# RWKV phase of a two-layer diffusion step: side work, piece copies and the first pair's rows placed anew

## What is computed

```
mod = silu(cond) @ w_ada + b_ada            # 6*D columns, per layer; "ada" chunks of 256 columns
h   = rms_norm(x, g_mix) * (1 + sc1) + sh1
p   = h @ w_in                              # its last 3*D columns are the branch gates
# RWKV-7, forward and backward, 8 heads of 64 (the reference's scan over time):
s   = s*w_t + (s a_t) b_t + v_t k_t ;  y_t = s r_t
gn  = group_norm(y_f + flip(y_b)) * lnx_w + lnx_b
o_c = (gn + bonus) * g_c
gates  = sigmoid(p[..., OFF_GATE:])         # 3 x D
merged = gates[0]*(o_a @ w_po_a) + gates[1]*(o_b @ w_po_b) + gates[2]*(o_c @ w_po_c)
x = x + gt1 * (merged @ w_out)
x = x + gt2 * (swiglu FFN of the normed x)  # uses sh2, sc2, gt2 of mod
```

## Time and profile before

| what | value |
|---|---|
| median of 3 runs | 1980.56 us |
| the profiled execution's own time | 1980.41 us |
| its span, and the mean granted TensorE clock | 1978.5 us, 0.963 |
| PE / DVE / ACT / POOL busy | 90% / 49% / 38% / 14% |
| chain that ended last: PE / DVE / ACT / issue | 74% / 13% / 6% / 4% |
| phase 3 of layer 0 and of layer 1, about | 394 to 637 us, 1364 to 1595 us |

### The profile page before, as it was taken

One profiled execution on the slowest core, in us unless ns is written; L12 is line 12 of the kernel. 1 busy time (PEld: TensorE's weight loads), 2 busy tenths in 40 slices (PEclk: granted clock), 3 DMA queues, 4 the chain that ended last, 5 costly groups with the idle time before them and its releaser, 6 DMA issues.

```text
span 1978.5 us, 42029 instructions
## 1 busy us (share of the span) xinstructions
PE 1781.8 (90%) x18403; PEld 1492.9 (75%) x18403; DVE 963.2 (49%) x1699; ACT 748.9 (38%) x1325; POOL 273.7 (14%) x457
## 2 busy tenths in 40 slices
PE   4899888778897999999989998987788989999998
PEld 2899555437664989999989984554566679899998
DVE  1526436576654463334342454375666446533332
ACT  2434435334335343333233434454333343533321
POOL 2000003265430000000000000052745000000000
PEclk9899998989898999999999999999799999999999
DMA  7443233201305445763442442321031443344342
GB/s 260 163 121 117 81 100 114 81 12 46 109 3 165 157 128 138 191 171 95 132 153 88 128 120 89 123 93 49 2 109 46 128 145 116 98 128 128 102 128 80
DMA packets 268525, 219.51 MB, mean 111 GB/s; under 512 B 7289, under 2 KB 259608, under 8 KB 267704
## 3 DMA queue, kind: packets, MB, share of 16 engines
q1 hardware_dynamic: 264816, 203.67, 34.2%
q0 software_dynamic: 3312, 13.09, 1.9%
q10 hardware_dynamic: 216, 0.06, 0.0%
HBM read 210.77 MB, written 6.03 MB: 110 GB/s over the span
## 4 chain that ended last, share of the span: by engine, by line
PE 74%; DVE 13%; ACT 6%; issue 4%; POOL 1%; DMA 1%; ACTq 0%; SPq 0%; DVEq 0%; POOLq 0%
PE bank L588 13%; PE bank L593 13%; PE bank L589 12%; PE bank L647 8%; PE bank L1256 3%; PE bank L1254 3%; PE bank L1255 3%; PE bank L1029 3%; PE bank L653 2%; PE bank L547 2%; PE bank L644 1%; PE bank L1038 1%; PE bank L774 1%; PE bank L811 1%; PE bank L572 1%
## 5 line engine op out<-in xcount | busy, mean ns | idle before, releaser
L589 PE MATMUL bank<-scr_rounded 128*128 128x384 f32 x1344 | 452.4, 337 | 0.0
L589 PEld LDWEIGHTS bank<-scr_rounded 128*128 128x128 f32 x1344 | 253.7, 189 | 1.3
L647 PE MATMUL bank<-h,ring 128*128 128x384 f32 x576 | 215.9, 518 | 31.0 <-ACT gtmp L1486 14.7
L588 PE MATMUL bank<-scr_rounded 128*128 128x384 f32 (+1 forms) x672 | 226.6, 337 | 13.9 <-ACT scr_rounded L1505 13.3
L588 PE MATMUL bank<-scr_rounded,gate_rounded 128*128 128x384 f32 (+1 forms) x672 | 228.0, 339 | 11.2 <-ACT scr_rounded L1505 9.3
L593 PE MATMUL bank<-scr_rounded,gate_rounded 128*128 128x384 f32 (+1 forms) x672 | 222.4, 337 | 0.0
L593 PE MATMUL bank<-scr_rounded 128*128 128x384 f32 (+1 forms) x672 | 221.9, 336 | 0.0
L1983 DVE TENSOR_TENSOR scr_rounded<-ring,gate_rounded 128x2048 fp32r<-128x2048 f32 (+3 forms) x65 | 135.4, 2083 | 153.3 <-ACT gate_rounded L1494 152.6
L1983 DVE TENSOR_TENSOR scr_rounded<-ring,scr_rounded 128x2048 fp32r<-128x2048 f32 (+1 forms) x65 | 135.4, 2083 | 137.9 <-ACT scr_rounded L1494 136.2
L647 PEld LDWEIGHTS bank<-h,ring 128*128 128x128 f32 x576 | 108.4, 198 | 108.9 <-issue 53.3
L1494 ACT ACTIVATE gate_rounded<-ring 128x2048 fp32r<-128x2048 f32 (+3 forms) x65 | 113.6, 1748 | 153.1 <-PE bank L593 64.6
(11 more groups left out here) (410 smaller groups left out, 3138.6 us busy)
## 6 DMA issues: line engine op xcount, KB each, us to landing
ring<-in_w_in_dram SPq DMA_DIRECT2D x56, 1024.0 KB, 5.3
ring<-in_w_ada_dram SPq DMA_DIRECT2D x48, 1024.0 KB, 5.4
ring<-in_w_ffn_in_dram SPq DMA_DIRECT2D x88, 512.0 KB, 5.2
ring<-in_w_ffn_out_dram SPq DMA_DIRECT2D x32, 704.0 KB, 4.5
ring<-in_w_out_dram SPq DMA_DIRECT2D x8, 1024.0 KB, 5.0
ring<-in_w_po_a_dram SPq DMA_DIRECT2D x4, 1024.0 KB, 5.9
ring<-in_w_po_b_dram SPq DMA_DIRECT2D x4, 1024.0 KB, 6.1
ring<-in_w_po_c_dram SPq DMA_DIRECT2D x4, 1024.0 KB, 9.4
```

What stands on the lines that cost most here:

```text
L588: pe.matmul(o, w_hi[:, k, :], right[0][k], start=k == 0, stop=False)
L589: pe.matmul(o, w_lo[:, k, :], right[0][k], start=False, stop=False)
L647: ins = pe.matmul(b[:, 0:T], w[:, k, 128 * (j % 2):128 * (j % 2) + 128], h[:, k, :], start=k == 0, stop=k == KD - 1)
```

## The change

Five edits. (1) `FILLS`: the place behind `loras` gets 2 steps instead of 4 and the one behind `grams(0)` 6 instead of 4, so that the second po item stands behind `grams(0)`; all places of the last pair (n = 3) get none, a new `fill(2)` stands between the mean and the variance of the last head pair, and what is left runs in `finish`. (2) `side_plan`: six modulation chunks (numbers 8 to 13 of the list `ada`) stand together behind po tile 3, the seventh (14) at the end of phase 3, and the eighth (15) in phase 4 behind the two gate tiles; before, four stood behind po tile 3 and four behind po tile 7. (3) POOL: the first pair's blocks and substitution come before its `factors`, and `own_blocks(0)` before `factors(2)` and `factors(3)`. (4) ACT: in `decays`, `side_work` comes before the wait for `rw_keys`. (5) DVE: the copy of the initial state (L2449) comes behind `terms(3)` instead of ahead of `logs(3)`.

```diff
--- before.py
+++ after.py
@@ -370,7 +370,7 @@
                     eng.wait_ge(phase[other], l * NPHASE + k + 1)
 
 
-        FILLS = (4, 4, 4, 4, 0, 0, 1, 1, 1, 1, 1, 1, 2, 1, 1, 0, 1, 1, 1, 1, 1, 1, 2, 1, 1, 0, 1, 1, 1, 1, 1, 1, 0, 1, 1, 0, 1, 1, 1, 1, 0, 0, 0)
+        FILLS = (4, 2, 6, 4, 0, 0, 1, 1, 1, 1, 1, 1, 2, 1, 1, 0, 1, 1, 1, 1, 1, 1, 2, 1, 1, 0, 1, 1, 1, 1, 1, 1, 0, 0, 0, 0, 0, 0, 0, 0, 0, 0, 0)
 
         def side_plan(l, k):
 
@@ -383,14 +383,15 @@
                 po = [po_of(0, j) for j in range(8)]
                 return po[0:4] + [ada[5]] + po[4:8] + [ada[6], gate_of(1, 0), gate_of(1, 1), ada[7]]
             if k == 4:
-                return [gate_of(2, j) for j in range(2)]
+                return [gate_of(2, j) for j in range(2)] + [ada[15]]
             plan = []
             for j in range(8):
                 plan.append(po_of(1, j))
                 if j < 6:
                     plan.append(gate_of(1, j + 2))
-                if j % 4 == 3:
-                    plan += ada[8 + j - 3:8 + j + 1]
+                if j == 3:
+                    plan += ada[8:14]
+            plan.append(ada[14])
             return plan
 
         def next_ada(l):
@@ -1219,6 +1220,7 @@
                         ins = turn(b[0:64, 128 * hp:128 * hp + 128], hfin[:, 4 * d + hp, :])
                     ins.then_inc(psum_ready, 1)
                 head_mean(3)
+                fill(2)
                 head_var(3)
                 finish(l, 3)
                 barrier(pe, "pe", l, 3)
@@ -1414,13 +1416,13 @@
                     gp.wait_ge(*last())
                     gp.tensor_tensor(pc[:, 4 + hp, :], both, pc[:, hp, :], mult).then_inc(*tells("rw_bonus"))
 
+                off_blocks(0)
+                substitution(0)
                 factors(0)
                 factors(1)
-                off_blocks(0)
-                substitution(0)
+                own_blocks(0)
                 factors(2)
                 factors(3)
-                own_blocks(0)
                 off_blocks(1)
                 substitution(1)
                 bonus_rows(0)
@@ -1713,9 +1715,9 @@
                 def decays(g):
 
                     hp, d = groups[g]
+                    side_work("wl", l, g)
                     if g:
                         act.wait_ge(S["rw_keys"], told("rw_keys", l, g))
-                    side_work("wl", l, g)
                     act.wait_ge(psum_ready, filled("wl", l, g))
                     b = bank("wl", l, g)
                     A(sg, b[:, 0:T], ACT.Tanh, bias=P(l, "w0", 4 * d + hp), scale=0.5).then_inc(*step())
@@ -2443,15 +2445,15 @@
                 logs(2)
                 keys(2)
                 unit_keys(2)
-                side_work("s0T", l)
-                dve.wait_ge(psum_ready, filled("s0T", l))
-                b = bank("s0T", l)
-                cp(h0.rearrange("p a b -> p (a b)"), b[:, 0:512]).then_inc(*empties("s0T", l))
                 logs(3)
                 terms(2)
                 keys(3)
                 unit_keys(3)
                 terms(3)
+                side_work("s0T", l)
+                dve.wait_ge(psum_ready, filled("s0T", l))
+                b = bank("s0T", l)
+                cp(h0.rearrange("p a b -> p (a b)"), b[:, 0:512]).then_inc(*empties("s0T", l))
                 grams(1)
                 inverses(0)
                 begin(1)
```

## The result

The changed kernel takes 1994.88 us (median of 4, 1992.81 to 1998.19) against 1981.05 us of before (4 runs): the ratio is 1.007, with a 95% interval of 1.0044 to 1.0095. It is slower by 0.7%, 14 us, where 6 us more were forecast. The profiled execution took 1994.98 us, its span is 1993.1 us at a mean clock of 0.957, 14.6 us longer than the span before.

A forecast was written before the change was run, and what follows sets the result against it. PE was taken to bound the kernel, with some 45 us of waits per layer in phase 3. Terms summed to -1.0 in layer 0 and -5.1 in layer 1, 6.1 us longer: 1986.5 us, range 1973 to 1999.

The forecast's parts named there:

- Start, +7.0: Start of phase 3: PE's 7.34 us stall on gate tile 3 goes, gaining 7.0 us per layer.
- the limit: Start of phase 3: POOL's second inverse, ready at about 462, is last and limits the gain to 6.2 to 9.7.
- DVE's cost beside POOL: Start of phase 3: POOL's factors slow DVE beside them; in the new order the pieces trade places, costed at nothing.
- Pairs 1 and 2, -2.5 and -0.5: Per layer, n = 1 loses 2.5 us to a late bank; n = 2 loses 0.5 to a merge ahead of DVE's transposes.
- The wait for chunk 13's bank: n = 1: half a po tile waits for ACT to empty the bank, starting at 536.5 instead of 533.7.
- Pair 3, +7.0 and +2.9 with the tail: n = 3 to the barrier: fills leave the last pair, the tail grows; gain 7.0 us in layer 0, 2.9 in layer 1.
- Start of phase 4, -12.0: PE waits 9.2 us for gate 10's landing and ACT's work behind it, then does chunk 15; 12.0 us lost per layer.
- (b): Slower by the clock: phase 4's main products start at 0.50, layer 0's pause only moves; 1997.6 us, chance 0.31.
- (a): Faster: whole start gain of +9.7, no wait in n = 1, phase 4 costs 10; 1968.7 us, chance 0.17.
- (c): Start of phase 3: gate tile 3's stall moves to the next tile, 7 less per layer; 2000.5 us, chance 0.05.
- The 2.0 us of a transfer: Start of phase 4: about 2.0 us fixed per DMA transfer, so splitting or hurrying it wouldn't bring the wait under that.

The follow-up runs named there:

- kernel 4: Kernel before with only the start's edits of FILLS, ACT and DVE, POOL's order left as before: 1963.96 us, ratio 0.9905.
- experiment 8: kernel 4 with the second half of po tile 7 later in the last pair, just ahead of the first modulation chunk: 1958.37 us, ratio 0.988.
- experiment 2: Changed kernel with ACT's side work at the start of phase 4 ahead of its split of gate 10: 1973.61 us, ratio 0.9961.
- experiment 6: Kernel before with the start's edits including POOL's new order, but ACT again waits for rw_keys ahead of its side work: 1981.42 us, ratio 1.0001.
- kernel 1: Changed kernel with modulation chunk 15 back at the end of phase 3, behind chunk 14: 1977.01 us, ratio 0.9977.
- Kernels 9 to 11: Start's edits, six chunks together, pair 1's po half later: 1959.45 us; same, POOL's old order: 1964.33; changed kernel with that half, POOL's old order, ACT's side work first: 1961.64.

## Why the prediction was right and where it was off

The direction, the range and the main mechanism (the wait at the start of phase 4) held; the sum was 6.1 us where 14 were measured. By the ledger 1.4 of the missing 8 us lie in layer 0, 5.5 in layer 1, where every term came out lower than forecast, and the rest outside the two stretches.

- **Start, +7.0.** 5.9 and 6.3 in the traces, 7.0 to 7.8 as a kernel by itself. Right in size, in part by luck, since the reason that I gave for the limit was half right: in the kernel after DVE's L2329 of pair 1 waits for POOL 0.7 us in layer 1 and not at all in layer 0 (460.56, POOL ended at 460.4), and kernel 4, which has the inverse 7 us earlier, is only 0.3 to 2.4 us better in the trace and not measurably so in time. DVE's cost beside POOL did trade places: with POOL's factors behind the substitution, L2318 and the two L2334 slowed (0.56 and 1.03 us before, 1.17 and 2.22 after), and L2297 fell from 1.34 to 0.72. One row was misread for it: at 432.28, where L2295 took 0.55, POOL stood idle (from 431.4 to 433.7), and beside the substitution it takes 0.72 to 0.75. The exchange wasn't free either: the first substitution, now beside DVE's terms, took 17.6 us instead of 15.4.
- **Pairs 1 and 2, -2.5 and -0.5.** The wait for chunk 13's bank was named, and is 3.77 us. Not counted was the clock behind it: L1098 took 2.54 instead of 1.62. In layer 1 the sum is -4.5; in layer 0 it is -2.0, as the kernel before had a pause of 1.96 us without a releaser in pair 1 there (to 524.68) and a low clock behind it, and the kernel after has not.
- **Pair 3, +7.0 and +2.9 with the tail.** Layer 0: 10.6 - 4.6 = 6.0. Layer 1: 5.8 - 4.6 = 1.2. The tail was 1 us longer than counted, because PE was at 0.50 in it (chunk 14 took 1.89, not 1.05). The pause in layer 0 shrank to 0.58 us, though the +7.0 only weighed its going against its moving; experiment 8 shows what it hangs on.
- **Start of phase 4, -12.0.** 12.3 and 13.6. The steps held one by one: 9.02 of wait (9.2 said), 1.89 for the chunk, 0.56, 0.69. The ring and ACT's order made the wait, as experiment 2 shows: with gate 10 as late, it goes when ACT's order is changed. What was left out is that in layer 1 the side gates took 12.0 us before (mean clock 0.72 in their first 5 us) and 13.3 after (0.50). Why the clock was lower for longer stays open: before, PE had stood 4.93 us in front of them, after, only 0.56, behind waits of 2.69 and 0.56 in the tail.
- **Rivals.** (b), the clock, makes up part of the missing 8 us, though mostly elsewhere than it said (the tail, pair 1, layer 1's side gates). Of its own terms the slow chunk and turn came (1.89 and 0.69), while gate 10's weights landed 5.2 us behind the side gates, as in the sum, the main products started slowly for only a few products (0.67 and 0.51 us, soon 0.33), and the pause in layer 0 didn't move. (a) did not come: its start of +9.7 wasn't reached (5.9 and 6.3), the wait in pair 1 was there, and phase 4 cost over 12, not 10. (c) did not come: po tile 1 is merged at 416.66, the tanh of gate tile 3 runs right behind it, and no gate tile of PE waits there.
- **The 2.0 us of a transfer.** What the prediction takes from the Trainium skill ("DMA: Bandwidth & Descriptors", Anatomy of one DMA) is given there for transfers that GpSimd issues; the ring's are issued by SyncE. No run here shows a fixed part, and no term of the sum rests on it.

## What to carry to other kernels

An engine that runs one program in order should never have work that another engine waits for behind a wait for something late: moving one such call was worth 21 us here (experiment 2), and another up to 16 (experiment 6). When a chunk moves in a ring of three slots, follow what its slot now waits for, not only where it is used. And time the edits apart: here those at the start gave 16 us, the others took 30 away, one (POOL's order) costs 7 us or nothing depending on another, and two effects of one more cancelled.

## What the runs showed of the hardware

PE can stand for 4 us with nothing to wait for, just past many short products, while weights come in at 350 GB/s. With the weights 7 us later against PE's program the pause was 1.25 us, and PE worked through a burst of the same rate (experiment 8; 5.6 us in 1964 by medians, at the edge of what these runs can tell). What it waits for is not shown.

The new waits also cost clock: behind 2.69 and 9.02 us of waiting PE was granted 0.50 (the 1.2 GHz level), behind 3.77 us a mean of 0.63 in the next 4.6 us, and what followed took 1 to 2 us longer. It isn't so each time: behind the same 2.69 us chunk 14 ran at full speed (1.05 us) in layer 0 of kernel 1 and in layer 1 of kernel 2.

The lowest median here is kernel 8's, 1958.4 us: the start's edits without POOL's, with the last po half moved. Kernels 9 to 11 can't be told from it by time.
